# Ten weight remainders of the up-projection, made on GpSimd in place of VectorE

## What is computed

```
pre = jnp.einsum('thkd,td->thk', u[expert], xb).astype(jnp.float32)
act = jax.nn.gelu(pre, approximate=False) * gate
return jnp.einsum('thk,thkd->td', act.astype(v.dtype), v[expert])
```

## Time and profile before

| | |
|---|---|
| median of 3 runs | 1863.45 us (1862.44 to 1866.87) |
| the profiled execution | 1860.44 us |
| its span, first to last instruction | 1858.6 us |
| PE busy | 1774.4 us, 95% |
| DVE busy | 1433.9 us, 77% |
| POOL busy | 647.2 us, 35% |
| up-projection, first matmul to last | 600.3 to 1266.1 us |

### The profile page before, as it was taken

One profiled execution on the slowest core, in us unless ns is written; L12 is line 12 of the kernel. 1 busy time (PEld: TensorE's weight loads), 2 busy tenths in 40 slices (PEclk: granted clock), 3 DMA queues, 4 the chain that ended last, 5 costly groups with the idle time before them and its releaser, 6 DMA issues.

```text
span 1858.6 us, 26358 instructions
## 1 busy us (share of the span) xinstructions
PE 1774.4 (95%) x9675; PEld 1517.5 (82%) x9675; DVE 1433.9 (77%) x2750; ACT 778.6 (42%) x1555; POOL 647.2 (35%) x409
## 2 busy tenths in 40 slices
PE   6999999889999899999989999978999999999997
PEld 6999766559999899999989999976676776766764
DVE  4432676764678888999999999867888878787787
ACT  3122466653444433443767888522222222222222
POOL 1100000000000033444233366556556556675662
PEclk8999799789999999999999999998999999999999
DMA  6233100002221599999888899999999999999995
GB/s 218 68 122 132 46 1 1 1 1 78 74 79 66 170 342 336 318 330 332 269 289 300 294 387 386 389 401 315 381 394 395 401 397 386 401 395 390 401 392 214
DMA packets 153599, 478.22 MB, mean 257 GB/s; under 512 B 14896, under 2 KB 53808, under 8 KB 149888
## 3 DMA queue, kind: packets, MB, share of 16 engines
q1 hardware_dynamic: 96112, 264.62, 38.8%
q0 software_dynamic: 56928, 208.28, 30.5%
q10 hardware_dynamic: 432, 3.64, 0.5%
HBM read 419.47 MB, written 56.75 MB: 256 GB/s over the span
## 4 chain that ended last, share of the span: by engine, by line
PE 76%; DVE 16%; DMA 3%; issue 2%; ACT 2%; POOL 1%; SPq 0%; ACTq 0%; DVEq 0%
PE ps L1003 22%; PE ps L981 16%; PE ps L633 10%; PE ps L1012 9%; PE ps L918 5%; DVE hot L1718 3%; PE ps L723 3%; DVE w_lo L1339 3%; DVE ring L1737 3%; DMA raw<-w_tiles 2%; PE ps L969 2%; PE ps L714 2%; PE ps L766 2%; DMA ring<-u_rows,idx_b 1%; PE ps L845 1%
## 5 line engine op out<-in xcount | busy, mean ns | idle before, releaser
L981 PE MATMUL ps<-md_hi,w_hi 128*128 128x384 f32 x1024 | 357.5, 349 | 26.9 <-DVE w_lo L1339 26.4
L981 PE MATMUL ps<-md_hi,w_lo 128*128 128x384 f32 x1024 | 345.2, 337 | 0.0
L981 PE MATMUL ps<-md_lo,w_hi 128*128 128x384 f32 x1024 | 345.0, 337 | 0.0
L613 POOL DMA_INDIRECT ring<-u_rows,idx_a x128 | 199.3, 1557 | 386.4 <-DVE dots L1737 276.8
L613 POOL DMA_INDIRECT ring<-v_rows,idx_a x128 | 226.2, 1767 | 130.1 <-DVE acc L1747 95.6
L1339 DVE TENSOR_TENSOR w_lo<-raw,w_hi 128x1024 fp32r<-128x1024 f32 x176 | 215.2, 1223 | 64.0 <-ACT w_hi L1265 44.0
L1737 DVE CUSTOM_DVE_ANT_0 ring<-ring,x_n 128x1024 f32<-128x1024 f32 x192 | 230.5, 1222 | 14.5 <-DMA ring<-u_rows,idx_b 12.8
L1747 DVE SCALAR_TENSOR_TENSOR acc<-ring,actg,acc 128x1024 f32<-128x1024 f32 x188 | 234.6, 1281 | 0.0
L981 PEld LDWEIGHTS ps<-md_hi,w_hi 128*128 128x128 f32 x1024 | 194.1, 190 | 34.7 <-DVE w_lo L1339 33.8
L1003 PE MATMUL ps<-w_hi,p_hi 128*128 128x512 f32 x576 | 193.7, 418 | 9.0 <-DVE w_lo L1805 9.0
L981 PEld LDWEIGHTS ps<-md_lo,w_hi 128*128 128x128 f32 x1024 | 194.2, 190 | 0.0
(11 more groups left out here) (265 smaller groups left out, 3262.0 us busy)
## 6 DMA issues: line engine op xcount, KB each, us to landing
raw<-w_tiles SPq DMA_DIRECT2D x176, 512.0 KB, 5.4
v_buf<-v_rows SPq DMA_DIRECT2D x128, 512.0 KB, 10.1
gates_scattered<-g_st SPq DMA_DIRECT2D x24, 1024.0 KB, 6.4
g_in<-gates_scattered SPq DMA_DIRECT2D x32, 768.0 KB, 15.1
activated<-act_st SPq DMA_DIRECT2D x112, 192.0 KB, 4.4
act_in<-activated SPq DMA_DIRECT2D x28, 768.0 KB, 11.3
kv_t<-qkv ACTq DMA_DIRECT2D x3, 1184.0 KB, 4.4
xh<-x_t SPq DMA_DIRECT2D x8, 296.0 KB, 6.7
```

The lines of the kernel that those rows point to most:

```text
L613: pool.indirect_dma_start(ring[slot][:], None, u_rows if table == "u" else v_rows, bass.IndirectOffsetOnAxis(ap=idx, axis=0)).then_inc(gat ...
L981: mm = nc.tensor.matmul(ps[:, slot, 0:ND], w[:, slot, kc, :], x[:, kc, :], start=(kc == 0 and j == 0), stop=(kc == KC - 1 and j == 2))
```

## The change

For ten tiles, 58, 62, 66 and so on to 94, DVE's `lo_part` is left out and POOL makes the same subtraction (`low_part`), on a semaphore of its own, `pool_split`. PE's wait for the remainder and SP's wait for the buffer go through `u_split`, which gives the semaphore and the count of the engine that makes a tile's remainder. POOL's instruction stands in its list just ahead of gather number `along(DOT_LINE, i - 1) + RING_U`, and it waits for ACT's rounded part.

```diff
+POOL_LOW = list(range(58, 97, 4))
...
+        pool_split = sem("pool_split")
...
+        def u_split(i):
+
+            if i in POOL_LOW:
+                return pool_split, POOL_LOW.index(i) + 1
+            return w_split, B_U + i + 3 - sum(j < i for j in POOL_LOW)
...
-                    sp.wait_ge(w_split, B_U + i - RAW_SLOTS + 3)
+                    sp.wait_ge(*u_split(i - RAW_SLOTS))
...
+            def low_part(i):
+
+                pool.wait_ge(hi_ready, B_U + i + 1)
+                nc.gpsimd.tensor_tensor(w_lo[:, (B_U + i) % 2], raw_u[i % RAW_SLOTS],
+                                        w_hi[:, (B_U + i) % 2].bitcast(F32), SUB).then_inc(pool_split, 1)
+
             for s, (table, blk, k) in enumerate(OPS):
+                for i in POOL_LOW:
+                    if s == along(DOT_LINE, i - 1) + RING_U:
+                        low_part(i)
...
-                pe.wait_ge(w_split, B_U + i + 3)
+                pe.wait_ge(*u_split(i))
...
-                if i + 1 < N_EXP:
+                if i + 1 < N_EXP and i + 1 not in POOL_LOW:
                     lo_part(B_U + i + 1, (i + 1) % 2, raw_u[(i + 1) % RAW_SLOTS])
```

## The result

| | median | runs from .. to |
|---|---|---|
| before, 22 runs | 1862.39 us | 1855.59 to 1868.05 |
| changed, 22 runs beside them | 1866.47 us | 1862.41 to 1877.61 |
| ratio changed to before | 1.0028 | 95% interval 1.0016 to 1.0040 |

By the ratio over the runs the changed kernel is 0.28% slower, 5.2 us with an interval of 3.0 to 7.4; the two medians alone differ by 4.1 us. The forecast was +7.0 us, and 1870.5 counted from the median of three runs, 1863.45. The profiled execution of the changed kernel has a span of 1864.0 us.

What follows compares the result with a forecast made beforehand. DVE was taken to set the pace from 882.6 to 1061.7, PE before and right after. Terms 3.8 + 2.0 + 1.2 = +7.0 us gave 1867.4 for the profiled execution, 1870.5 against the median; range 1863 to 1875.

Steps and rivals of the forecast that it cites:

- POOL's length: Duration of POOL's 128x1024 subtraction, taken as 2.4 us from estimates of 2.52 and 2.23 us.
- Tile 58: Where PE sets the pace: POOL's remainder, behind a gather, comes 1.3 or 2.5 us late; 1.9 taken.
- The race: At tile 58, POOL's start at 855.85 against DVE's dot product at 855.82: 1.3 or 2.5 us late.
- Tile 62, with the stall of 61: POOL, behind two gathers, 2.2 us late at tile 62; a stall of 0.3 us at tile 61 won.
- Tiles 66 to 90: In DVE's stretch: -8.0 us of remainders, 4 x 2.4 = 9.6 blocked, 0.4 at 90; +2.0 in all.
- what PE loses there it would have stood later for DVE: At tile 78, POOL's lateness (ready 976.8, PE at 974.69 after 1.37 of stall) was not added.
- The gathers that leave later: Gathers behind POOL's instruction leave up to 4.8 us later; issued 15 us or more ahead, costed at nothing.
- Tile 94: Behind DVE's stretch: two gathers, then a dot product, make POOL's remainder late: +1.2 us (1.0 to 2.4).
- The first rival: POOL reads beside DVE, nothing blocked; net -0.9 up to +3, about +1 us, 1864.5; chance 0.25.
- The second rival: POOL's instruction takes no more than 1.2 us, so DVE's 8.0 us are won: 1855.5; chance 0.08.
- The third: PE's gaps from 1188 to 1266 swallow the shift, +7 shrinks to nothing: 1863.5; chance 0.10.

Runs made afterwards that it cites:

- POOL's work beside alone: Kernel before, DVE keeping all remainders, plus a POOL subtraction of constants into an unread buffer at the ten places; +13.23 us at tile 92, untimed.
- the one with 70 and 74: Against the kernel before, only the remainders of tiles 70 and 74 made on POOL; shift -2.27 us at tile 92, untimed.
- the early one: Changed kernel with its ten POOL subtractions one iteration earlier in POOL's list; shift +6.53 us at tile 92 against the kernel before, untimed.
- the one with 66, 78, 82 and 86: Against the kernel before, only the remainders of tiles 66, 78, 82 and 86 made on POOL; shift +4.79 us at tile 92, untimed.
- selects: Against the kernel before, remainders of tiles 68, 70, 71, 72 and 74 made on POOL, ahead of select steps; shift -5.22 us at tile 92, untimed.
- singles: Against the kernel before, remainders of tiles 68, 70, 71, 72, 74, 77, 79, 81, 87 made on POOL; 1855.06 us against 1860.26, ratio 0.9972.
- only 58, 62: Against the kernel before, only the remainders of tiles 58 and 62 made on POOL; shift +3.03 us at tiles 65 and 95, untimed.

## Why the prediction was right, step by step

**POOL's length.** 2.4 us forecast; 2.38 at tile 58, where nothing held it, 2.53 on the mean. Right.

**Tile 58** (forecast +1.9, from 1.3 or 2.5). The race that I left open went POOL's way:

```profile
852.18 0.94 POOL L632 DMA_INDIRECT ring<-u_rows,idx_a  x1 [0.30 <-issue]
853.15 2.38 POOL L615 TENSOR_TENSOR w_lo<-raw,w_hi 128x1024 fp32r<-128x1024 f32 x1
...
853.06 3.57 DVE L1756 CUSTOM_DVE_ANT_0 ring<-ring,x_n 128x1024 f32<-128x1024 f32 x1
...
855.59 0.44 PE L1000 MATMUL ps<-md_hi,w_hi 128*128 128x384 f32 x1 [1.09 <-POOL w_lo L615]
```

The gather takes 0.94 as foreseen and POOL starts 0.03 us after it. The dot product's row begins 0.09 us earlier than POOL's, and yet it is the one that is held, for 2.35 us; DVE had that room, it stood 0.36 us for ACT after it. A shift of 1.25, and 1.36 by the next tile. The forecast's term, a middle between two ends, was 0.5 too large.

**Tile 62, with the stall of 61** (forecast +1.9). 3.01 - 1.36 = +1.65; PE stood 1.90 us:

```profile
874.44 0.44 PE L1000 MATMUL ps<-md_hi,w_hi 128*128 128x384 f32 x1 [1.90 <-POOL w_lo L615]
```

**Tiles 66 to 90** (forecast +2.0, bounds -8.0 and +6.8). 4.79 - 3.01 = +1.78. The kind of step that decides is the one named, tile by tile: held at 66, 78, 82 and 86, free at 70 and 74, 0.35 at 90. That the size is right as well is in part luck: two parts of it were off, and they offset each other. The four holds are 2.14 to 2.19 us, not 2.4: 8.7 + 0.35 - 8.0 = +1.0. And at tile 78 "what PE loses there it would have stood later for DVE" did not hold to the end:

```profile
973.45 2.50 POOL L615 TENSOR_TENSOR w_lo<-raw,w_hi 128x1024 fp32r<-128x1024 f32 x1
...
973.67 4.50 DVE L1737 TENSOR_TENSOR hot<-cst,rt_t 128x1024 f32<-128x1024 f32 x2
...
976.01 0.44 PE L1000 MATMUL ps<-md_hi,w_hi 128*128 128x384 f32 x1 [2.58 <-POOL w_lo L615]
```

After that stall PE ran the tile at half its clock and lost 1.57 us more (78 to 79 in the table). DVE then stood 0.54 us for ACT at 985, and at tile 91, where PE had stood 1.48 us for DVE before, it does not stand for DVE at all. So I read the last 0.7 of this term as PE's lateness come through after all; DVE's 0.54 is seen, the rest is argued. PE also stood for POOL at 86 (0.85 us) and 90 (0.59), which the forecast did not name. The gathers that leave later, put at nothing, cost nothing: DVE stood for no gather from 845 to 1090, only for ACT.

**Tile 94** (forecast +1.2). 5.99 - 4.79 = +1.20. The second of two gathers ends at 1074.60, DVE's dot product at 1074.92; the next dot product is held:

```profile
1072.63 1.97 POOL L632 DMA_INDIRECT ring<-u_rows,idx_a  x1 [0.30 <-issue]
1074.62 2.53 POOL L615 TENSOR_TENSOR w_lo<-raw,w_hi 128x1024 fp32r<-128x1024 f32 x1
...
1074.85 3.40 DVE L1756 CUSTOM_DVE_ANT_0 ring<-ring,x_n 128x1024 f32<-128x1024 f32 x1
...
1077.21 0.45 PE L1000 MATMUL ps<-md_hi,w_hi 128*128 128x384 f32 x1 [0.93 <-POOL w_lo L615]
```

**The sum.** +7.0 forecast, +5.99 measured at tile 95; 0.5 of the difference is the race, 0.3 tile 62, 0.2 the stretch of 66 to 90.

**The first rival, that DVE is not blocked,** is out: 3.41 us beside POOL, and +13.23 from POOL's work beside alone. The rule of the Trainium skill ("SBUF — State Buffer", Who interferes with whom) agrees with these rows on the side that the trace of before left open: DVE, second to issue, waits for POOL (at tile 58, with the rows 0.09 us apart, their starts do not tell which issued first). **The second rival, POOL in time,** is out by its waits. **The third, that the gaps from 1188 on swallow the shift,** is not borne out: +5.99 at tile 113 stands beside +5.2 (3.0 to 7.4) in the timed runs, -6.64 beside -5.2 (-9.9 to -0.6). Single executions differ there, though. After tile 113 the shifts of a trace wander by up to 5 us and more: the changed kernel has +9.61 at tile 127 and +8.04 at its end, the one with 70 and 74 has -1.67 and -2.06, the early one +7.13 and +12.62, the one with 66, 78, 82 and 86 +6.48 and +11.66. The two winners lost most of their gain there in the execution that was traced: selects -3.57 and -0.86, singles -6.01 and -1.42. So only repeated runs speak for the whole time, and of the experiments only the singles had them. What makes the stretches with a DMA share of 1.00 differ from one execution to the next I did not look into.

## What to carry to other kernels

Before work is handed to an idle engine, look at what stands in its queue ahead of it and what released that: POOL was free two thirds of the time, and still 1 to 2.6 us late, because gathers stood there that DVE's dot products released. Where VectorE and GpSimd both read SBUF, moving 1.14 us from one to the other cost the first 2.2 us wherever its next instruction read two tensors, and nothing where it read one (a copy apart, see below). So choose the places by what the other engine does just then: the same instruction in nine places, seven of them new, turned a loss of 6.0 us into a gain of 6.6 in this stretch.

## What the hardware showed that I had not expected

**A held VectorE instruction looks busy.** In the profile the wait for POOL is no idle time: the instruction's row is longer (3.41 in place of 1.22) and starts before POOL's ends. Busy shares hide it; the mean of a group shows it. Dot products from 882.6 to 1055 in the changed kernel, against 1.22 us before:

```profile
L1756 DVE CUSTOM_DVE_ANT_0 ring<-ring,x_n 128x1024 f32<-128x1024 f32 x32 | 43.1, 1359 | 0.6
```

**A copy of one tensor was held too.** At 1051.00 a DVE copy of 128x128 that took 0.23 us in the kernel before took 0.58, until just after POOL's end at 1051.50, while the two sums before it, also with one input, ran at their length. What sets the copy apart no run here tells. The rows of the changed kernel:

```profile
1049.76 1.21 DVE L1688 TENSOR_REDUCE routed<-eqs_high 128x64 f32<-128x1024 f32 x1
1051.00 0.58 DVE L1692 COPY routed<-c 128x128 f32<-128x128 f32 x1
```

**The clock after a stall.** After PE's 2.58 us at tile 78 the granted clock of 977 to 980 was 0.50, the lower of the two levels (1.2 of 2.4 GHz); after 2.01 us at tile 65 of the same execution it stayed at 1.00 (windows of the changed kernel; the eighth column, after POOL's count, is the clock):

```profile
889.30:892.80 3.50, 3.50 (x23) 3.50 (x24) 3.50 (x5) 2.71 (x8) 2.19 (x2) 1.00 0.80 244
977.00:980.00 3.00, 3.00 (x14) 3.00 (x13) 3.00 (x10) 2.88 (x9) 0.86 (x1) 0.50 0.84 269
```

And after the same stall of 2.02 us at tile 65 it fell in the kernel with the five select places (window of that kernel):

```profile
886.50:890.00 3.50, 3.50 (x18) 3.50 (x19) 3.50 (x5) 2.71 (x8) 1.69 (x1) 0.71 0.84 249
```

From tile 57 to 95 it fell eight times in the nine kernels of the table, after stalls of 2.01 to 3.59 us; other stalls of 2.01 to 2.31 us left it at 1.00. Six times the tile took 1.55 to 1.59 us longer (78 to 79 in two columns of the table, 65 to 66 in four). Twice, at tile 72 in "only 58, 62" and "early", only 0.20 to 0.25 us of it is left by tile 73, where PE's 1.12 us stall for DVE went away. So a stall of some 2 us costs itself or itself and up to 1.6 more, and its length alone does not tell which.
